# First B/C and dt projection of a Mamba-2 layer taken from the raw residual, and a new load order for the last two experts

## What is computed

```python
def rmsnorm(x, w):
    y = xf * lax.rsqrt(jnp.mean(xf * xf, axis=-1, keepdims=True) + RMS_EPS)
    return (y * w)

def mamba2_mixer(h, in_proj, conv_w, conv_b, dt_bias, a_log, d_skip, norm_w, out_proj):
    proj = h @ in_proj
    z = proj[..., :D_INNER]
    xbc = proj[..., D_INNER:D_INNER + SSM_CONV_DIM]
    dt_raw = proj[..., D_INNER + SSM_CONV_DIM:]
    xbc = jax.nn.silu(causal_dwconv(xbc, conv_w) + conv_b)
    dt = jax.nn.softplus(dt_raw + dt_bias)
    ...
def expert_block(args):
    hb = jax.nn.silu(xb @ w_gate[e]) * (xb @ w_up[e])
    return hb @ w_down[e]
...
h = h + mamba2_mixer(rmsnorm(h, norm_mix[1]), ...)
h = h + hierarchical_moe(rmsnorm(h, norm_ffn[1]), ...)
```

## Time and profile before

| | us |
|---|---|
| median of 3 runs | 1379.08 |
| lowest and highest of them | 1378.95 and 1379.86 |
| the profiled execution | 1377.48 |
| its span in the trace | 1375.7 |
| TensorE busy | 1076.4 (78% of the span) |
| VectorE busy | 460.7 (33%) |
| ScalarE busy | 243.8 (18%) |
| read from memory | 465.68 MB |

### The profile page before, as it was taken

The page is one execution under the profiler, slowest core; times in us unless marked ns, Lnnn a source line. Parts: engine busy times, 40 slices in busy tenths (PEclk is TensorE's granted clock), DMA queues, the critical chain, the costliest instruction groups (busy, mean ns, idle before and its releaser), DMA issues.

```text
span 1375.7 us, 21346 instructions
## 1 busy us (share of the span) xinstructions
PE 1076.4 (78%) x9316; PEld 724.1 (53%) x9319; DVE 460.7 (33%) x1163; ACT 243.8 (18%) x556; POOL 6.9 (1%) x28
## 2 busy tenths in 40 slices
PE   8999786757757667779999999887776585676774
PEld 7888543433424244348888888644434252343532
DVE  2251452322222222234655555463222122222123
ACT  2220111111111111122433333211111111111002
POOL 1000000000000000000000000000000000000000
PEclk9999998878878787889999999989788787887788
DMA  9753599999999999964656663469999999999994
GB/s 347 237 213 170 219 429 427 425 428 428 426 427 428 426 427 428 425 222 123 199 199 224 232 237 117 197 270 426 427 427 427 426 427 427 426 428 427 427 404 181
DMA packets 87942, 468.15 MB, mean 340 GB/s; under 512 B 16941, under 2 KB 56105, under 8 KB 62889
## 3 DMA queue, kind: packets, MB, share of 16 engines
q1 hardware_dynamic: 87344, 466.11, 83.5%
q10 hardware_dynamic: 504, 0.67, 0.1%
HBM read 465.68 MB, written 1.08 MB: 339 GB/s over the span
## 4 chain that ended last, share of the span: by engine, by line
PE 38%; issue 35%; DMA 23%; DVE 2%; ACT 1%; SPq 0%; POOL 0%; DVEq 0%; POOLq 0%; ACTq 0%
DMA w_gu<-in_expert_w_up 23%; PE pb L1175 10%; PE pa L1175 7%; PE acc L1199 4%; PE pa L1413 3%; PE acc L1301 2%; PE wa L1413 2%; PE wb L1422 2%; PE pb L1230 1%; PE pb L1404 1%; ACT arena L447 1%; PE wa L1182 1%; PE acc L1432 1%; PE wb L1587 1%; PE pb L1391 0%
## 5 line engine op out<-in xcount | busy, mean ns | idle before, releaser
L1413 PE MATMUL pa<-w_gu,arena 128*32 128x256 f32 x1536 | 130.5, 514 | 92.6 <-DMA w_gu<-in_expert_w_up 92.6
L961 DVE TENSOR_SCALAR arena<-arena 128x128 f32<-128x128 f32 x64 | 14.5, 226 | 481.2 <-ACT arena L447 481.2
L1413 PE MATMUL wa<-w_gu,arena 128*32 128x256 f32 x1344 | 99.4, 461 | 64.8 <-DMA w_gu<-in_expert_w_up 63.2
L1413 PEld LDWEIGHTS pa<-w_gu,arena 128*32 128x32 f32 x1536 | 60.5, 146 | 168.0 <-DMA w_gu<-in_expert_w_up 104.9
L447 ACT ACTIVATE arena<-wb 32x256 f32<-32x256 f32 (+2 forms) x262 | 98.5, 376 | 121.8 <-PE wb L1422 117.3
L1175 PE MATMUL pb<-hnT,w_x 128*128 128x256 f32 x512 | 113.3, 379 | 2.4 <-DVE arena L1007 2.4
L1413 PEld LDWEIGHTS wa<-w_gu,arena 128*32 128x32 f32 x1344 | 48.4, 132 | 115.6 <-DMA w_gu<-in_expert_w_up 72.3
L1175 PEld LDWEIGHTS pb<-hnT,w_x 128*128 128x128 f32 x512 | 96.5, 190 | 15.6 <-issue 2.8
L1404 PE MATMUL pb<-arena,hs 128*128 128x128 f32 x480 | 79.7, 334 | 31.1 <-issue 15.1
L1404 PEld LDWEIGHTS pb<-arena,hs 128*128 128x128 f32 x480 | 73.5, 242 | 45.4 <-issue 41.4
L1422 PE MATMUL wb<-w_dn,arena 128*32 128x256 f32 x1440 | 87.3, 384 | 4.0 <-DVE arena L943 2.7
(11 more groups left out here) (276 smaller groups left out, 1190.0 us busy)
## 6 DMA issues: line engine op xcount, KB each, us to landing
w_dn<-in_expert_w_down SPq DMA_DIRECT2D x45, 2048.0 KB, 26.7
w_gu<-in_expert_w_gate SPq DMA_DIRECT2D x45, 2048.0 KB, 30.9
w_gu<-in_expert_w_up SPq DMA_DIRECT2D x45, 2048.0 KB, 35.4
arena<-in_expert_w_down SPq DMA_DIRECT2D x20, 2048.0 KB, 27.2
w_x<-in_expert_w_gate SPq DMA_DIRECT2D x20, 2048.0 KB, 31.4
w_x<-in_expert_w_up SPq DMA_DIRECT2D x20, 2048.0 KB, 35.9
w_x<-in_odd_in_proj SPq DMA_DIRECT2D x16, 1024.0 KB, 5.4
w_x<-in_odd_in_proj SPq DMA_DIRECT2D x16, 512.0 KB, 5.5
```

Source lines behind the costliest of these rows:

```text
L961: link(v.tensor_scalar(eg, eg, 1.0, None, ALU.add))
L1413: ins = mm(gu[32 * j:32 * j + 32, :, :], xb[:, k, c0:c0 + CAP], w_gu[s][:, :, k, P * j:P * j + P], start=(k == 0), stop=(k == KC - 1))
```

## The change

Two edits.

**Load order.** In expert_stream, the last two experts' pages go out as gate and up of 30, gate and up of 31, down of 30, down of 31. Before it was gate, up, down of 30, and then gate, up, down of 31. Each page keeps its own wait.

**Mixer C's opening.** Before the residual additions of layer 0's experts, DVE multiplies the norm weights into the dt weights (128x256) and into the first B/C weights in w_x (128x2048, after waiting for their landing, c2_in). TensorE then takes B of group 0 and dt from resT itself, part by part as the residual is finished, with the sums of squares put between: dt goes to partitions 0 to 31 of wb, the sum of squares to partition 32. C of group 0 is taken from resT in pieces (raw_c) put between the steps of the norm's chain. ACT copies the 33 rows, TensorE turns them over with two transposes, and DVE makes dt from the turned result with the token's factor and the bias in one operation per tile. hnT is made as before. x of group 0 comes first from it (its first half follows hnT tile by tile, its second half stands behind the cumulative sums). The token's factor is spread to the other half of wb, ACT copies it to rg, and DVE multiplies it into B and C in pa (semaphore bc0_norm) before the first tap.

```diff
--- before.py
+++ after.py
...
@@ -323,8 +323,14 @@
                     if e == OV_AT + 2:
                         k1 = sp_.value_load(table[0:1, l + 1:l + 2], min_val=0, max_val=OV_LIST)
                         sp_.wait_ge(S["ov_done"], k1 + 1)
+                    if e == NE - 2:
+                        break
                     for part in range(3):
                         expert_part(l, e, part, NE * l + previous(e))
+                for parts in ((0, 1), (2,)):
+                    for e in (NE - 2, NE - 1):
+                        for part in parts:
+                            expert_part(l, e, part, NE * l + previous(e))
 
             def late_params():
                 sp_.dma_start(nffn[:, :, :], norm_ffn.rearrange("l (p k) -> p l k", k=KC)).then_inc(S["par_wr"], 16)
@@ -617,9 +623,11 @@
                 sigmoid(ecv).then_inc(S["x1_exp"], 1)
 
             def odd_bc_tap(g):
-                act.wait_ge(S["bc_done"], g + 1)
                 if g:
+                    act.wait_ge(S["bc_done"], g + 1)
                     act.wait_ge(S["x1_silu"], g)
+                else:
+                    act.wait_ge(S["bc0_norm"], 1)
                 first_tap(pa2, [g + 16, g + 24]).then_inc(S["bc_tap"], 1)
 
             def odd_bc(g):
@@ -641,13 +649,15 @@
                 act.wait_ge(S["h_part"], 5 + b)
                 af(hsq[:, 2 * b:2 * b + 2, :], resT[:, 2 * b:2 * b + 2, :], ACT.Square).then_inc(S["sq_part"], 1)
             act.wait_ge(S["ss_done"], 1)
-            af(msR, wb[0:1, 0:SEQ], ACT.Copy).then_inc(S["ss_copied"], 1)
+            af(dsR, wb[0:HEADS + 1, 0:SEQ], ACT.Copy).then_inc(S["ss_copied"], 1)
             act.wait_ge(S["par_head"], 4 * 16)
             act.wait_ge(S["dt_pre"], 1)
             chain.link(af(dta, dtv, ACT.Abs))
             chain.link(af(dta, dta, ACT.Exp, scale=-1.0))
             af(dta, dta, ACT.Ln, bias=one_c[:, :]).then_inc(S["dt_ln"], 1)
             af(w0, alog[:, :], ACT.Exp).then_inc(S["alog_exp"], 1)
+            act.wait_ge(S["hn_in"], KC)
+            af(rg, wb[:, SEQ:], ACT.Copy).then_inc(S["row_copied"], 1)
             odd_bc_tap(0)
             act.wait_ge(S["cum_done"], 1)
             af(csT[:, :], wa[0:HEADS, 0:SEQ], ACT.Copy).then_inc(S["cs_copied"], 1)
@@ -981,6 +991,14 @@
                         with dve.If(k0 < k1):
                             with dve.Fori(k0, k1) as k:
                                 overflow(k, l)
+                if l == 0:
+                    dve.wait_ge(S["par_head"], 4 * 16)
+                    v.tensor_tensor(wdt[:, :, :], wdt[:, :, :],
+                                    norm_w[:, 1, :].unsqueeze(2).to_broadcast([P, KC, HEADS]), ALU.mult)
+                    dve.wait_ge(S["c2_in"], 32)
+                    w0_c = w_c[2].rearrange("p k a b -> p k (a b)")
+                    v.tensor_tensor(w0_c, w0_c, norm_w[:, 1, :].unsqueeze(2).to_broadcast([P, KC, 2 * P]), ALU.mult
+                                    ).then_inc(S["w0_scaled"], 1)
                 for c in range(4):
 
                     dve.wait_ge(S["comb_part"], NE * (l + 1) + c + 1)
@@ -996,10 +1014,16 @@
 
 
             dve.wait_ge(S["ss_t"], 1)
-            v.tensor_scalar(st[:, 5, :], wa[:, 0:TT], EPS, None, ALU.add).then_inc(S["mean_sq"], 1)
+            ds2 = wa[:, 0:64 * TT].rearrange("p (t b) -> p t b", t=TT)
+            v.tensor_scalar(st[:, 5, :], ds2[:, :, HEADS], EPS, None, ALU.add).then_inc(S["mean_sq"], 1)
+            dve.wait_ge(S["rstd"], 2)
+            for t in range(TT):
+                ins = v.scalar_tensor_tensor(dtv[:, t, :], ds2[:, t, 0:HEADS], st[:, 4, t:t + 1], dtb[:, :],
+                                             ALU.mult, ALU.add)
+            ins.then_inc(S["dt_pre"], 1)
             dve.wait_ge(S["row_done"], 1)
             for k in range(KC):
-                v.scalar_tensor_tensor(hnT[:, k, :], resT[:, k, :], norm_w[:, 1, k:k + 1], pb[:, 0:SEQ],
+                v.scalar_tensor_tensor(hnT[:, k, :], resT[:, k, :], norm_w[:, 1, k:k + 1], wb[:, SEQ:],
                                        ALU.mult, ALU.mult).then_inc(S["hn_in"], 1)
 
             def odd_z(g):
@@ -1032,17 +1056,18 @@
                 dve.wait_ge(S["bc_exp"], g + 1)
                 v.tensor_tensor(bcT, cv, ecv, ALU.mult).then_inc(S["bc_silu"], 1)
 
-            dve.wait_ge(S["par_head"], 4 * 16)
-            for q in range(2):
-                v.tensor_copy(dskip[64 * q:64 * q + 64, :], skip_row[64 * q:64 * q + 64, q:HEADS:2])
-            dve.wait_ge(S["dt_raw"], 1)
-            v.tensor_tensor(dtv, acc[:, 0:TT, 0:HEADS],
-                            dtb[:, :].unsqueeze(1).to_broadcast([P, TT, HEADS]), ALU.add).then_inc(S["dt_pre"], 1)
+            dve.wait_ge(S["dt_pre"], 1)
             dve.wait_ge(S["dt_ln"], 1)
             link(v.scalar_tensor_tensor(dtv, dtv, 0.0, dta, ALU.max, ALU.add))
             dve.wait_ge(S["alog_exp"], 1)
             link(v.tensor_tensor(dta, dtv, w0.unsqueeze(1).to_broadcast([P, TT, HEADS]), ALU.mult))
             v.tensor_scalar(dta, dta, -1.0, None, ALU.mult).then_inc(S["dt_a"], 1)
+            dve.wait_ge(S["bc_done"], 1)
+            dve.wait_ge(S["row_copied"], 1)
+            v.tensor_tensor(pa2, pa2, rg.unsqueeze(1).to_broadcast([P, 2, SEQ]), ALU.mult).then_inc(S["bc0_norm"], 1)
+            for q in range(2):
+                v.tensor_copy(dskip[64 * q:64 * q + 64, :], skip_row[64 * q:64 * q + 64, q:HEADS:2])
+            dve.wait_ge(S["bc0_norm"], 1)
             odd_bc_taps(0)
             dve.wait_ge(S["cum_done"], 1)
             cum = wb[:, 0:TT * HEADS].rearrange("p (t n) -> p t n", t=TT)
...
@@ -1528,30 +1543,47 @@
                 project(pb[:, 0:SEQ], w_c[0], 0)
                 project(pb[:, SEQ:], w_c[0], 1).then_inc(S["z1_done"], 1)
 
-            for k in range(KC):
-                if k % 2 == 0:
-                    pe.wait_ge(S["sq_part"], 5 + k // 2)
-                ins = mm(wb[0:1, 0:SEQ], esum[:, NG + NE:], hsq[:, k, :], start=(k == 0), stop=(k == KC - 1))
+            def raw_c(ks):
+                for k in ks:
+                    ins = mm(pa[:, SEQ:], w_c[2][:, k, 1, :], resT[:, k, :], start=(k == 0), stop=(k == KC - 1))
+                return ins
+
+            pe.wait_ge(S["w0_scaled"], 1)
+            for b in range(4):
+                pe.wait_ge(S["h_part"], 5 + b)
+                for k in (2 * b, 2 * b + 1):
+                    mm(pa[:, 0:SEQ], w_c[2][:, k, 0, :], resT[:, k, :], start=(k == 0), stop=(k == KC - 1))
+                pe.wait_ge(S["sq_part"], 5 + b)
+                for k in (2 * b, 2 * b + 1):
+                    mm(wb[0:HEADS, 0:SEQ], wdt[:, k, :], resT[:, k, :], start=(k == 0), stop=(k == KC - 1))
+                    ins = mm(wb[HEADS:HEADS + 1, 0:SEQ], esum[:, NG + NE:], hsq[:, k, :],
+                             start=(k == 0), stop=(k == KC - 1))
             ins.then_inc(S["ss_done"], 1)
+            raw_c((0, 1))
             pe.wait_ge(S["ss_copied"], 1)
             for t in range(TT):
-                ins = mm(wa[:, t:t + 1], msR[:, P * t:P * t + P], one_c[0:1, :], start=True, stop=True)
+                ins = nc.tensor.transpose(wa[:, 64 * t:64 * t + HEADS + 1], dsR[:, P * t:P * t + P],
+                                          ident[0:HEADS + 1, 0:HEADS + 1])
             ins.then_inc(S["ss_t"], 1)
+            raw_c((2, 3, 4, 5))
             pe.wait_ge(S["rstd"], 2)
             for t in range(TT):
-                ins = mm(pb[:, P * t:P * t + P], st[:, 4, t:t + 1].to_broadcast([P, P]), ident[:, :], start=True, stop=True)
+                ins = mm(wb[:, SEQ + P * t:SEQ + P * t + P], st[:, 4, t:t + 1].to_broadcast([P, P]), ident[:, :],
+                         start=True, stop=True)
             ins.then_inc(S["row_done"], 1)
-            pe.wait_ge(S["par_head"], 4 * 16)
-            by_tile([acc[:, t, 0:HEADS] for t in range(TT)], wdt).then_inc(S["dt_raw"], 1)
-            odd_bc(0)
+            raw_c((6, 7)).then_inc(S["bc_done"], 1)
+            zero_acc()
+            pe.wait_ge(S["c1_in"], 16)
+            for k in range(KC):
+                pe.wait_ge(S["hn_in"], k + 1)
+                mm(pb[:, 0:SEQ], w_c[1][:, k, 0, :], hnT[:, k, :], start=(k == 0), stop=(k == KC - 1))
             pe.wait_ge(S["dt_a"], 1)
+            pe.wait_ge(S["row_copied"], 1)
             for t in range(TT):
                 mm(wb[:, HEADS * t:HEADS * t + HEADS], upper[:, :], dta[:, t, :], start=True, stop=True)
                 mm(wa[0:HEADS, P * t:P * t + P], dta[:, t, :], upper[:, :], start=True, stop=True)
             mm(wb[:, 64:96], ones[:, :], dta[:, 0, :], start=True, stop=True).then_inc(S["cum_done"], 1)
-            pe.wait_ge(S["dt_pre"], 1)
-            zero_acc()
-            odd_x(0)
+            project(pb[:, SEQ:], w_c[1], 1).then_inc(S["x1_done"], 1)
             odd_bc(1)
 
             def odd_scores(g):
```

18 lines of the change are left out of this document (5 added, 13 removed).

## The result

The kernel with the change takes 1367.06 us (median, 1365.07 to 1368.24), the kernel before 1379.47 beside it. The ratio is 0.9908, interval 0.9891 to 0.9925: 12.4 us are gone, where 15.3 were forecast. The profiled execution took 1365.07 with a span of 1363.3, so the two traces differ by 12.4 too.

The account below looks back on a forecast made before the run. Transfers were taken to bound the expert loops, TensorE mixer C. Gains of 4.35 and 3.79 us (load order) and 7.2 (opening) sum to 15.3: 1379.08 - 15.3 = 1363.7 us, range 1361.5 to 1368.5.

Parts of the forecast that it names:

- Load order, landings: Ends of the expert loops: up of 31 lands one page (4.87 us) sooner, down of 31 stays last and releases its matmuls.
- from there both tails are unchanged: After the last down matmuls start, both layers' tails run as before, keeping gains of 4.35 and 3.79 us.
- the 9.34 us: Layer 0's tail: time from gate and up of 31 to down of 31 before the change, taken as the same after.
- Rival 2: Clock falls again: waits near 595 and 599 bring a half-clock stretch into the opening, 3.3 us lost, 1367.0; chance 0.12.
- The opening: Mixer C, from the combine's end to the scores: 29.85 us in place of 37.03, a gain of 7.2 us.
- The eight changes of width: Opening: TensorE's switches between full width and 32 columns cost 0.5 us in all, bounded by 0 and 2.7.
- C stands in the norm's gaps, and dt costs nothing of its own: Opening: the stated source of its 7.2 us gain, part of it going back as a 1.3 us wait.
- The scaling: DVE's scaling of B/C weights before the residual additions costs nothing, hidden by the combine with 1 us of cover.

Follow-up runs that it names:

- e8: The kernel with the change timed again, unchanged, with more rounds: 1368.19 us, ratio 0.9900.
- e3: The kernel with the change plus eight 128-column matmuls with unused results ahead of expert 31's down matmuls: 1365.65 us, ratio 0.9898.
- e6: The kernel with the change plus eight unused matmuls ahead of expert 31's down, and all of B ahead of all dt/squares pairs: 1363.73 us, ratio 0.9877.
- e5: The kernel with the change, but C of group 0 in one piece after the norm factor's spread, not in the norm's gaps: 1367.19 us.
- e4: The kernel with the change, but dt's and the squares' matmuls kept apart by B's, so none run side by side: 1371.26 us, ratio 0.9933.
- e7: The kernel with the change, but the scaling of the first B/C weights done three times on DVE, twice by one: 1368.94 us.
- e9: The kernel with the change plus unused matmuls in each router, 18 ahead of the ranks and 7 ahead of the first gather: 1361.34 us, ratio 0.9869.

## Why the prediction was right, and where it was off

The forecast was 1363.7, the measured median 1367.06, which the range from 1361.5 to 1368.5 holds; e8's 1368.19 is held only just. The gain was put at 15.3 for 12.4, nearly a quarter too high. Step by step:

- **Load order, landings: right.** One page sooner, the last page last, down of 31 released by a transfer, 19.88 us after gate and up of 30 for a forecast of 19.69. In layer 1 the gain is 3.82 for 3.79.
- **Load order, "from there both tails are unchanged": this step failed** in layer 0. The gain there is 2.57 for 4.35. Of the difference 0.2 is the page, 1.6 the down matmuls at 1.2 GHz (3.52 us for 1.93), and the filler of e3 gives it back. I had carried over the price of down of 31 from a row where it ran right behind busy work. Half clock was in this tail before as well: gate and up of 31 took 5.91 us after an idle 5.50, 3.66 at full clock in layer 1 of the kernel after. There it stood within the 9.34 us that I took over whole, and the down matmuls came once it had passed, behind an idle 0.66. Now they stand behind an idle wait of their own, and the clock, back at 1.00 from 594.00 to 597.90, falls a second time. That layer 1 gave all of its 3.79 is partly luck: in e8 the same fall is there.
- **Rival 2 was right in kind and wrong in place.** It named the waits near 595 and 599 and looked for their effect in the opening, at 3.3 us. The clock fell directly behind the first wait, in the tail, at 1.6 us, and was full from 606.80 on; no trace with the new opening has a stretch at half clock in it.
- **The opening: right.** Counted from the combine's end, forecast and measured: squares done 7.5 and 7.97, spread ended 11.5 and 11.64, hnT done 14.7 and 14.9, TensorE ready for the scores 28.5 and 28.75, its wait 1.3 and 1.31, scores 29.85 and 30.07. VectorE goes from taps to silu without waiting for the decay rows, as forecast.
- **The eight changes of width: mis-sized,** 0.5 for about 1. In the chain a group of two pairs takes 0.98, four of them 3.92, where e6's eight pairs in one run take 3.57: three changes into narrow groups fewer, 0.12 each. B behind a group takes 1.06 where it takes 0.86: 0.20 for a change back. Three of each make the 0.95 that e6 saved up to the last square. The Trainium skill, "TensorEngine Tiling (Array Packing)", Key Properties, says that a mode change drains TensorE and that tiles operate independently: the traces agree with both, at 0.1 to 0.2 us a change and with a pair at the price of one.
- **"C stands in the norm's gaps, and dt costs nothing of its own": not the whole reason.** e5 shows that the gaps themselves give 0.2 us. What gives the 7 us is that B, C and dt no longer wait for hnT, with dt at no price (some 3.5 us, e4), and that the stretch at half clock is gone, 3.4 us by the trace before. The forecast held this last part without naming it: it set an old opening with the stretch, 37.03 us as measured, against a new one priced at full clock throughout. The size came out right with half of its cause unsaid. That early B, C and dt are what keeps the clock up is argued, not tested.
- **The scaling: right,** with a cover of 2.8 us (e7) rather than 1, because the combine ended at 606.79 where I had it at 604.10.
- **The rest of the miss.** The first 578 us are 0.91 longer in the trace after, in code that the change doesn't touch; from the ranks to the first gate and up of layer 0 alone 9.56 us for 8.97. And the median stands 2.0 above the profiled execution for the 1.6 that I assumed. With 1.8 from the tail and 0.2 from the opening that is 3.3 of the 3.4 us.

What stays open is what sets the spread of 3 to 5 us between runs of the kernel after. A part is the length of the stretches at 1.2 GHz behind the router's idle time, and whether down of 31 runs at half clock in the last tail, as two traces show. The Trainium skill, "TensorE: Matmul & The Clock Gate", Part 1, says that the gate watches on a schedule of its own, not bound to the program, so that the same kernel can run slow for more or fewer matmuls. The two traces agree, with 3.06 us and 1.95 us for the same sixteen instructions; and so do the last down matmuls of layer 1, with 3.38 us and 1.93 us behind waits of 1.87 and 1.88; but e9, without the router's idle stretches, spreads by 3.7 us too. Open as well is what decides, at one and the same wait, whether the clock falls.
